# Staging nine of twelve weight slots of an MoE stage, and summing the outputs of the experts in PSUM

## What is computed

```python
logits = x2 @ w_router + b_router
top_vals, top_idx = lax.top_k(logits, TOP_K)          # 4 of 32
gates = jax.nn.softmax(top_vals, axis=-1)
# for each expert e and the rows xb that chose it
gu = xb @ w_up[e] + b_up[e]
gate, up = gu[:, :D_EXPERT], gu[:, D_EXPERT:]
gate = jnp.minimum(gate, SWIGLU_LIMIT)
up = jnp.clip(up, -SWIGLU_LIMIT, SWIGLU_LIMIT)
act = (up + 1.0) * (gate * jax.nn.sigmoid(SWIGLU_ALPHA * gate))
out = act @ w_down[e] + b_down[e]                     # times the gate, summed per token
y = rmsnorm(x + moe(rmsnorm(x, norm_ffn_g)), norm_final_g)
```

## Time and profile before

| | us |
|---|---|
| median of 3 runs | 1290.15 |
| range of the runs | 1289.37 to 1290.32 |
| span of the profiled execution | 1288.5 |

### The profile page before, as it was taken

The page is one execution under the profiler, slowest core; times in us unless marked ns, Lnnn a source line. Parts: engine busy times, 40 slices in busy tenths (PEclk is TensorE's granted clock), DMA queues, the critical chain, the costliest instruction groups (busy, mean ns, idle before and its releaser), DMA issues.

```text
span 1288.5 us, 30593 instructions
## 1 busy us (share of the span) xinstructions
PE 1174.2 (91%) x11113; PEld 577.5 (45%) x11114; DVE 605.2 (47%) x1256; ACT 249.7 (19%) x487; POOL 467.4 (36%) x833
## 2 busy tenths in 40 slices
PE   8999999999999899798979998989989799899876
PEld 7777777775434333233323433433333233233232
DVE  2999983122644344354343442444524244444243
ACT  2012124001222122122212221212211122122112
POOL 1022300000444435445451454454444444535451
PEclk9999999999999999999989999999999999999997
DMA  9983442344899999999998799999999999999996
GB/s 260 337 269 119 144 135 105 129 155 166 334 385 399 421 421 422 421 421 421 422 421 364 307 398 422 420 422 421 422 421 421 421 421 421 422 421 408 421 421 254
DMA packets 94570, 448.97 MB, mean 348 GB/s; under 512 B 8526, under 2 KB 42894, under 8 KB 45339
## 3 DMA queue, kind: packets, MB, share of 16 engines
q1 hardware_dynamic: 93742, 446.55, 86.5%
q10 hardware_dynamic: 749, 1.19, 0.3%
q0 software_dynamic: 48, 0.85, 0.2%
HBM read 447.00 MB, written 2.42 MB: 349 GB/s over the span
## 4 chain that ended last, share of the span: by engine, by line
PE 55%; DMA 15%; DVE 13%; POOL 6%; issue 6%; SPq 3%; ACT 1%; DVEq 0%; POOLq 0%; ACTq 0%
PE banks L1369 20%; DMA ring<-in_w_down 15%; PE banks L1379 12%; DVE R L800 8%; PE banks L1164 8%; POOL ring L530 6%; PE banks L1086 4%; PE banks L1144 3%; PE banks L1123 2%; PE banks L1280 2%; SPq L398 1%; PE banks L1130 1%; PE banks L1153 1%; DVE R L809 1%; DVE R L812 0%
## 5 line engine op out<-in xcount | busy, mean ns | idle before, releaser
L1369 PE MATMUL banks<-ring,hT 128*32 128x512 f32 x3328 | 430.4, 611 | 62.3 <-POOL ring L530 57.5
L530 POOL COPY ring<-big 128x512 f32<-128x512 f32 x248 | 146.9, 641 | 554.4 <-SPq L404 554.4
L530 POOL COPY ring<-R 128x512 f32<-128x512 f32 x496 | 289.9, 631 | 113.4 <-DMA R<-in_w_up 113.4
L321 DVE TENSOR_TENSOR xt<-xt,banks 128x1024 f32<-128x1024 f32 x106 | 128.7, 1215 | 403.7 <-PE banks L1144 403.7
L1379 PE MATMUL banks<-ring,hT 128*32 128x256 f32 x3328 | 227.4, 392 | 18.4 <-DMA ring<-in_w_down 13.2
L1379 PEld LDWEIGHTS banks<-ring,hT 128*32 128x32 f32 x3328 | 107.5, 113 | 202.8 <-issue 123.3
L1164 PE MATMUL banks<-hT,ring 128*128 128x288 f32 x768 | 189.2, 407 | 0.2 <-ACT hT L554 0.2
L1369 PEld LDWEIGHTS banks<-ring,hT 128*32 128x32 f32 x3328 | 95.5, 111 | 195.6 <-POOL ring L530 81.1
L1164 PEld LDWEIGHTS banks<-hT,ring 128*128 128x128 f32 x768 | 145.7, 191 | 39.9 <-issue 0.3
L680 ACT COPY WT<-banks 128x256 f32<-128x256 f32 x52 | 19.4, 373 | 498.2 <-PE banks L1379 498.2
L800 DVE SCALAR_TENSOR_TENSOR R<-big,convw,R 128x256 f32<-128x256 f32 x240 | 108.1, 525 | 0.0
(11 more groups left out here) (252 smaller groups left out, 757.2 us busy)
## 6 DMA issues: line engine op xcount, KB each, us to landing
ring<-in_w_down SPq DMA_DIRECT2D x128, 1024.0 KB, 11.0
R<-in_w_up SPq DMA_DIRECT2D x124, 1024.0 KB, 18.1
ring<-in_w_up SPq DMA_DIRECT2D x70, 1024.0 KB, 9.4
big<-in_w_up SPq DMA_DIRECT2D x62, 1024.0 KB, 12.7
ring<-in_w_in SPq DMA_DIRECT2D x24, 1024.0 KB, 10.3
ring<-in_w_branch_b SPq DMA_DIRECT2D x4, 1024.0 KB, 4.9
ring<-in_w_branch_a SPq DMA_DIRECT2D x4, 1024.0 KB, 4.9
ring<-in_w_out SPq DMA_DIRECT2D x4, 1024.0 KB, 4.9
```

The lines of the kernel that those rows point to most:

```text
L321: nc.vector.tensor_tensor(dst, dst, rows, ALU.add).then_inc(y_added, 1)
L530: ins = nc.gpsimd.tensor_copy(ring[:, k, h * 512:(h + 1) * 512], parked[k][:, h * 512:(h + 1) * 512])
L1369: ins = mm(UP[g * BLK:(g + 1) * BLK, :], xT[:, k, :], ring[:, k, g * 512:(g + 1) * 512], start=k == 0, stop=k == UP_SLOTS - 1)
```

## The change

Five things change together.

1. `parked` grows from 6 to 9 slots (up 0 to 7 and down 0). To make room, `stage`, the mixer's buffers and the nine slots are packed in one region, `arena`. The buffers that would be overwritten last in the mixer lie last in it.
2. Parked slots 0 to 4 of place 1 are issued once the spatial gating has ended (`sp_evac`) and the chunk output is stored, ahead of the loads for place 0. Slot 5 follows the fourth of these, slots 6 and 7 follow `ya_evac`, and slot 8 comes after the down slots of place 0.
3. A round of SyncE's queue is reordered. Each parked slot is issued again as soon as its copy allows, with the other releases in between; parked slots 0 to 6 of the next expert now stand ahead of the direct down slots 9, 10 and 11 of this one, parked slot 7 behind slot 9, parked slot 8 at the end.
4. The outputs of all items are summed in PSUM: `clear_total` writes zeros with four matmuls in the first item, `combine` accumulates into `total`, and VectorE adds the totals into `xt` once, in the last item. The per-item add of the sample rows stays.
5. As `xt` no longer changes in the loop, the gather reads it directly, and the row scale moves into the 0/1 selection matrix `sel`. In the routing, the mean square of a row is found by VectorE (`bn_stats`, `bn_aggr` and one combination) in place of a ScalarE square, and the scaled copy into `stage` goes. Small GpSimd constants are made later.

```diff
-PARKED = 6
+PARKED = 9
+EARLY_SLOTS = 5
+ARENA = PARKED * SLOT + D
...
+            sp.wait_ge(sp_evac, 2 * G)
+            sp.wait_ge(v_stored, 16)
+            for k in range(EARLY_SLOTS):
+                load_parked(1, k)
             for k in range(UP_SLOTS):
                 sp.wait_ge(*mix_block_used(MIX_BLOCKS - SLOTS + k))
                 load_slot(0, k)
+                if k == 3:
+                    load_parked(1, EARLY_SLOTS)
             sp.wait_ge(ya_evac, 2 * KC)
-            for k in range(PARKED - 1):
+            for k in range(EARLY_SLOTS + 1, PARKED - 1):
                 load_parked(1, k)
...
+            def next_weights(place, here, after, before):
+
+                release_parked(before, range(0, 3))
+                load_parked_again(place + 1, after, (0,))
+                release_parked(before, (3,))
+                load_parked_again(place + 1, after, (1,))
+                release_parked(before, (4,))
+                load_parked_again(place + 1, after, (2,))
+                release_parked(before, (5, 6))
+                load_parked_again(place + 1, after, (3,))
+                release_parked(before, (7,))
+                load_parked_again(place + 1, after, (4, 5, 6))
+                release_parked(before, range(UP_SLOTS, PARKED))
+                load_direct(here, before, (PARKED,))
+                load_parked_again(place + 1, after, (7,))
+                load_direct(here, before, range(PARKED + 1, SLOTS))
+                load_parked_again(place + 1, after, (8,))
...
-            release_parked(before)
-            load_up_rest(here, before)
-            load_down(here, before)
+            release_parked(before, range(PARKED))
+            load_direct(here, before, range(PARKED, SLOTS))
...
+            def clear_total():
+
+                for q in range(QN):
+                    row = slice(q * BLK, (q + 1) * BLK)
+                    mm(high[:, q, :].rearrange("p (h n) -> p h n", h=2), zeros[row, :],
+                       slot_ids[row, 0:256].unsqueeze(1).to_broadcast([BLK, 2, 256]), start=True, stop=False)
...
-                combine_before(i)
+                combine_before(i, False)
...
                     if k == 6:
                         pe.wait_ge(combT_ready, i + 2)
                         pe.wait_ge(out_ready, i + 1)
-                        pe.wait_ge(y_added, i * NT + NT)
-                        combine(0, row_out[0])
+                        combine(0, total[0], False, False)
...
-                add_before(i, 2)
+                add_before(i)
                 dve.wait_ge(combT_turned, i + 1)
                 select_weighted(column1)
                 dve.wait_ge(gathered, i + 2)
                 select(column2)
-                add_before(i, 1)
-                dve.wait_ge(combined, i * NT + (NT + 1))
-                add_output(dve, row_out[0], 0)
```

More of the change, by code:

```diff
@@ new lines, in hybrid_layer @@
+        parked = [arena[:, k * SLOT:(k + 1) * SLOT] for k in range(PARKED)]
+        stage = region(NT * D).rearrange("p (t d) -> p t d", t=NT)
+        spb = region(G * P).rearrange("p (g i) -> p g i", g=G)
+        xs_rows = spb[0:NS].rearrange("p g i -> p (g i)")
+        big = region(KC * CB)
+        tmpc = region(2 * T).rearrange("p (h t) -> p h t", h=2)
+        WS = region(G * NS)[0:NS].rearrange("p (g i) -> p g i", g=G)
+        glu_tail = region(KC * NS).rearrange("p (c t) -> p c t", c=KC)
@@ L144, in view @@
+        convw = region(KC * W).rearrange("p (c k) -> p c k", c=KC)
+        mean_w = region(P)
+        vecrows = region(P)[0:8 * KC]
+        bmask = region(DB)[0:NS]
+        rep4 = region(DB * DS)[0:DS].rearrange("p (b t) -> p b t", b=DB)
+        region(EARLY_SLOTS * SLOT - taken[0])
+        R1, R2, R4, R3 = (region(KC * T) for _ in range(4))
+        fing = arena[:, PARKED * SLOT:PARKED * SLOT + D]
         def view(t, c):
@@ L381, in _, with weights, load_parked @@
                 load_block(n)
+            def weights(e, k):
+                if k < UP_SLOTS:
+                    return a["w_up"][0, bass.ds(e, 1), k * P:(k + 1) * P, :].rearrange("e p n -> (e p) n")
+                j = k - UP_SLOTS
+                return a["w_down"][0, bass.ds(e, 1), j * 256:(j + 1) * 256, :].rearrange("e (p h) n -> p (e h n)", p=P)
             def load_slot(e, k):
+                sp.dma_start(ring[:, k, :], weights(e, k)).then_inc(slot_full[k], 16)
+            def load_parked(e, k):
+                sp.dma_start(parked[k], weights(e, k)).then_inc(parked_full[k], 16)
@@ L395, in load_parked @@
-            def load_parked(e, k):
-                src = a["w_up"][0, bass.ds(e, 1), k * P:(k + 1) * P, :].rearrange("e p n -> (e p) n")
-                sp.dma_start(parked[k], src).then_inc(parked_full[k], 16)
-            def release_parked(before):
-                for k in range(PARKED):
-                    sp.wait_ge(up_used, before * UP_SLOTS + (k + 1))
+                    sp.wait_ge(up_used, before * UP_SLOTS + (k + 1))
+                else:
+                    sp.wait_ge(down_used, before * DOWN_SLOTS + (k - UP_SLOTS + 1))
@@ L404, in release_parked, with load_direct @@
+            def release_parked(before, ks):
+                for k in ks:
+                    wait_used(k, before)
                     sp.sem_inc(released, 1)
-            def load_up_rest(e, before):
-                for k in range(PARKED, UP_SLOTS):
-                    sp.wait_ge(up_used, before * UP_SLOTS + (k + 1))
+            def load_direct(e, before, ks):
+                for k in ks:
+                    wait_used(k, before)
                     load_slot(e, k)
-            def load_down(e, before):
-                for j in range(DOWN_SLOTS):
-                    sp.wait_ge(down_used, before * DOWN_SLOTS + (j + 1))
-                    load_slot(e, UP_SLOTS + j)
@@ L907, in add_mixed @@
                 V.tensor_tensor(dst, dst, bank[4 + 2 * tt + h][:, :], ALU.add).then_inc(x2_ready, 1)
+                dve.wait_ge(x2_ready, 2 * tt + h + 1)
+                link(V.bn_stats(bnst[:, tt, h, :], dst))
+                if h == 1:
+                    link(V.bn_aggr(mv[:, tt, :], bnst[:, tt, :, :]))
+                    V.scalar_tensor_tensor(ss[:, tt:tt + 1], mv[:, tt, 0:1], mv[:, tt, 0:1], mv[:, tt, 1:2],
+                                           ALU.mult, ALU.add).then_inc(squared2, 1)
             def keep_rows(tt):
@@ L964, in _ @@
             counts, count = bank[4][0:NE, 2 * NE:3 * NE], DN[0:NE, 0:1]
-            V.scalar_tensor_tensor(key_row, counts, float(NE), key_bias[:], ALU.mult, ALU.add)
+            V.scalar_tensor_tensor(key_row, counts, float(NE), key_bias, ALU.mult, ALU.add)
             link(V.scalar_tensor_tensor(key_col, count, float(NE), item_ids[0:NE, :], ALU.mult, ALU.add))
@@ L1139, in turn_rows, with combine @@
                 ins.then_inc(rows_turned, 1)
-            def combine(tt, rows):
+            def clear_total():
[3 more added lines that the diff above has]
+                       slot_ids[row, 0:256].unsqueeze(1).to_broadcast([BLK, 2, 256]), start=True, stop=False)
+            def combine(tt, rows, start, stop):
                 for q in range(QN):
```

203 lines of the change are left out of this document (91 added, 112 removed).

## The result

The changed kernel takes 1337.85 us in the median (1335.22 to 1344.78), the kernel before beside it on the same chip 1289.76 us: ratio 1.0385, 95% interval [1.0366, 1.0403]. Forecast were 1285.4 us and a range up to 1290.8 us. The change is slower by 48 us, over ten times the 4.3 us of the slower rival.

A forecast was written before the change was run, and what follows sets the result against it. Transfers at 421 GB/s were taken to set the pace. A 10.0 us lead of the loads, half given back to TensorE's tail, left 4.75 us: span 1283.75 plus 1.65 gave 1285.4 us, range 1281.2 to 1290.8 us.

The forecast's parts named there:

- the slower rival: VectorE blocked by GpSimd's copies at full price, and loads halting again at six two-item pairs; 1294.4 us, chance 0.12.
- Contention: GpSimd's longer copying reaches over the next item's VectorE chain; 0.5 us per first item of a place.
- c: TensorE's lateness at each first item of a place: forecast 0.5 us, by rows 1.7, slower rival decides from 1.2.
- Reordered queue: Down slot 11 stands behind eight parked loads; in a starved place it lands 15 us further back in the queue.
- The loads stand still again at the end of each pair: Within the slower rival: loads halt after pairs of two-item places; six pairs at up to 0.5 us, 3 us.
- Three more slots, earlier restart: Loads further on whenever buffers are full: 7.5 us by three staged slots, 6.3 us by SyncE issuing again earlier.
- TensorE-bound tail: After the last down-slot wait in place 29, TensorE's own work, 45.35 us, outlasts the transfers; it ends at 1271.85 us.
- The tie in that tail: Last item: GpSimd's slots ready after 26.2 us, TensorE wants the last at 26.5 us; 1.1 us added.
- the rival "same": GpSimd eats the gain through slower copies in the end chain and contention of 0.8 us; 1289.0 us, chance 0.19.
- Clearing the totals: Four new matmuls between up 3 and up 4 of the first item, on TensorE's path; 1.1 us, bounds 0.6 to 1.4.
- Removed adds, routing: Some 126 us of VectorE adds go, costed at nothing; routing's mean square moves to VectorE, cost 0, bounds -0.3 and +0.5.
- New sags in the six pairs: Sign that the forecast is wrong, pointing to the slower rival: transfer rate dips at the six pairs of two-item places.

The follow-up runs named there:

- e7_gap5: Changed kernel plus one gap per place: GpSimd waits for its own last copy after the sixth slot (slot 5); 1295.23 us, ratio 1.0044.
- e2_order: Changed kernel, nine staged slots kept, with the queue order of the kernel before; 1319.74 us, ratio 1.0234.
- e10_order_gap5: Changed kernel, nine staged slots, with the queue order of the kernel before and GpSimd's gap after slot 5; 1293.18 us, ratio 1.0029.
- e5_mix: Changed kernel with a gap after each slot and a mixed queue order, five staged loads ahead of down slots 9 to 11; 1286.33 us, ratio 0.9975.
- e1_drain: Changed kernel plus a gap after every slot: GpSimd waits for its own last copy before the next slot; 1296.47 us, ratio 1.0045.
- e12_six_mix: Changed kernel with six staged slots and a mixed order, five staged loads ahead of down slots 8 to 11; 1286.38 us, ratio 0.9978.
- e3_six: Changed kernel with six staged slots and the queue order of the kernel before, other parts of the change kept; 1288.87 us, ratio 0.9990.

## Why the prediction was wrong

**Contention: the step that failed.** I took 0.5 us for each first item of a place from the one row that had copies beside it. Measured are 4.2 us of VectorE and 2.1 us of TensorE's clock per hold, at eleven places. Not all of it reaches the end: the eleven cost 43 us together (changed kernel against e7_gap5), 3.9 us each. The five where the buffers are full cost 5.3 us each (e2_order against e10_order_gap5). That leaves some 2.7 us for each of the six in stretches where the transfers are short as well, an estimate from these two differences, whose orders of the queue differ. The text had the place right (GpSimd's copies "now reach over the next item's VectorE chain"), and the rival that turned on it had the right quantity: c above 1.2 us decides. But it let c end at 1.7 us, three operations waiting for one copy each. I added 6.9 us of copies per expert and didn't ask which instruction would be first in them, nor how narrow the margin was: the earlier trace rows ends at 367.21 + 8.97 = 376.18 us and the limit starts at 376.30 us. That alone would not have given the price. The row at 345.14 us stands 12.7 us into a run of 24 copies, as late as the later holds, and took 0.81 us; the limit at 344.01 us, 11.6 us into it, took 0.58 us. What those rows couldn't show is the copies of the changed kernel, whose records grow along a run where those of the kernel before don't. The prediction has no term for the packed region, and the growing records go with it in every run. Whether it is their cause is not shown.

**The page I cited.** The changed kernel's rows show one VectorE instruction waiting for 4.45 us beside the end of 32 copies, and another, early in a run, for 0.68 us. "SBUF — State Buffer", section "Who interferes with whom", in the Trainium skill says that the one that comes second is fully blocked for the whole instruction of the other. By that rule a hold is one copy, whose records last 0.61 to 0.79 us; the late arrivals stand some eight copies long, and there the measurement decides. The same section of the Trainium skill also names `tensor_scalar` in its two-port modes as one that contends with GpSimd, beside instructions with two SBUF inputs. I had used only the latter; the limit is a `tensor_scalar`, and the trace agrees that it can wait (0.68 us where 0.29 is free).

**Reordered queue.** "The loads stand still again at the end of each pair" was given 3 us within a rival and nothing in the forecast. With holds away, the transfers pause for 13 us over these stretches, TensorE waits 39.6 us for down slots where it waits 19.9 us in e5_mix, and the order costs 10 us (e1_drain against e5_mix). The step counted how far slot 11 moves back, and did not follow the queue through a pair of two-item places, where the place of the down slots decides how soon it can run on.

**Three more slots, earlier restart.** The lead at the transfers came out in e5_mix, with another order: its last weight lands at 1268.5 us, against 1275.5 before, 7.0 us earlier where 10.0 were forecast. That it is not worth that much at the end was forecast too, by the TensorE-bound tail. The tie in that tail, taken at 1.1 us, is what the rival "same" named: TensorE waits 3.9 us for GpSimd's copies in the last item. e5_mix and e12_six_mix, with and without the three slots, give the same time. Nine slots with before's order lose 4.3 us to six. The number 1285.4 lies near e5_mix's 1286.3, but that kernel has another order and gaps and the terms differ in it, so the nearness is luck.

**Steps that held.** Clearing the totals took 1.14 us, forecast 1.1 (the row: four matmuls of two passes, 32 by 512, at 333.57 us). Removed adds, routing, packed region and early loads together cost nothing (e3_six, 0.9990), apart from what part the packed region may have in the holds. The loop's first `up` starts at 330.0 us, against 331.2 before, and at 330.1 to 332.7 us in eleven of the experiments' kernels, which have the same routing, so no gain is shown there. VectorE's busy time fell by 116 us in e12_six_mix (605.2 to 489.0), forecast 125; the new `bn_stats` are in it. In the changed kernel it fell by 67 only, as a held instruction counts as busy: a high busy time can be a wait.

**The checklist.** Of the signs named, the first already failed: instead of 421 GB/s from about 400 us the windows show 403 over 415 to 700 us and 394 over 752 to 1160 us. "New sags in the six pairs" is what the page shows. It pointed at the slower rival, but to its mechanism only the timeline of VectorE led.

## What to carry to other kernels

Before an engine's run of copies is made longer, look up in the trace which instruction of its neighbour comes next after the run's present end, and how narrow the margin is. When its buffers are moved too, compare the records of single copies in both kernels before a price is taken over from the old trace. A long gapless series on GpSimd beside VectorE work in SBUF wants a pause where that work arrives; a wait on its own semaphore did it, and nine per expert cost no more than one (1293.47 and 1293.18 us). Weights that arrive earlier pay only as far as a copy and TensorE's own tail can follow: here 3 MB more of staging brought nothing, and the place of the down slots in the queue most of the 3 us that were won.

## What the runs showed of the hardware

- A VectorE instruction from SBUF to SBUF that arrives 7.6 to 13.6 us into GpSimd's gapless copies (0.55 us apart) can stand until the last of them ends: 4.45 to 5.5 us in the changed kernel, with 32 copies in the run. Arriving 3.4 us into a run, it takes 0.7 us, one copy. Some arrivals 5.8 to 12.7 us into a run also passed, in 0.41 to 0.58 us. An instruction that reads PSUM took its free 0.41 to 0.42 us in the same place. Whether a hold lasts longer still in longer runs was not tried.
- Within such a run the copies start 0.550 us apart while their records grow from 0.61 to 0.79 us, so that they overlap more and more. The limit is held when the copy it meets overlaps the one before it by 0.140 us or more, and not up to 0.134 us. In the kernel before the copies start 0.557 us apart, the overlap stays near 0.06 us, and a limit 11.6 us into a run passes in 0.58 us. Why the copies out of the packed region follow each other faster was not tested.
- The pause can be tiny: in e7_gap5 the trace shows all 36 copies as one group of 20.82 us, 0.58 us each, and yet the limit passes in 0.73 us (at 379.31 us). The copy behind the pause starts 0.805 us after the one ahead of it instead of 0.550.
- After an idle time of 4.05 us TensorE's granted clock was 0.55 in the following 5 us, and the work up to `up 2` took 2.1 us longer, half as much again as the hold itself.
